# A decoder layer with grouped experts on one core: expert rows in blocks of 32 instead of 64

## The chip, the cores and the metric

The kernel runs on one core of a Trainium2 chip. One launch computes the whole layer for one sequence of 512 positions, all in fp32. The metric is the device time of that launch in microseconds (us); lower is better. Three runs of the kernel before are given.

Engines: PE is TensorE (its weight loads are shown apart, as PEld), DVE is VectorE, ACT is ScalarE, POOL is GpSimd, and SP is SyncE, which here issues the loads of the weights.

## The reference, cut to what matters

The layer is a mixer (attention heads of several kinds) followed by a mixture of experts. The change lies in the second part: each of the 512 rows is sent to two of 16 experts of one group.

```python
def grouped_moe(u, w_router, w1, w3, w2):
    aff = softmax(xt @ w_router)                       # 512 x 16
    group_score = top_k(aff by groups of 4, 2).sum(-1)
    g_sel = argmax(group_score)                        # one of 4 groups
    top_w, top_i = top_k(aff inside the group, 2)      # two experts, weights sum to 1
    ...
    for e in range(16):
        h = silu(xt @ w1[e]) * (xt @ w3[e])            # 1024 -> 512
        y = y + gate[:, e:e + 1] * (h @ w2[e])         # 512 -> 1024
x = x + g2 * grouped_moe(rms_norm(x, norm2) * (1 + sc2) + sh2, ...)
```

There are 1024 pairs of a row and an expert. Each expert has three matrices, w1 and w3 of 1024 x 512 and w2 of 512 x 1024, 6.29 MB together.

## The kernel before, in words

The first 557 us of the launch are the modulation, the input projection, the attention branches, the output projection and the router. They are the same in both kernels, but for the shape of one copied tile (gate2).

The expert stage starts when DVE has counted how many rows each expert gets. Experts get whole blocks of BT = 64 rows, at least one block each; `block_start` holds the running number of blocks, and `expert_rows` in DRAM holds the rows by expert, with room for padding. GpSimd scatters the normalised rows there. Then all engines walk over the blocks, in loops whose bounds are read from `block_start` at run time. For one block g:

- ACT's queue loads the rows into `xg` (64 partitions, one buffer) by `xg_load`, line 633.
- PE transposes `xg` in 8 pieces into banks 4 and 5 (`xg_T`, line 1516); DVE and ACT copy four pieces each into `xgT`, with the scale and shift of the modulation (lines 1148 and 639).
- First product (`inner`, line 1523): the 64 rows are the stationary operand, so a product fills only half of the array's columns. Two products, h = 0 and 1, go to column tiles at partitions 0 and 64 and take different columns of w1 and w3. It is done in two halves s, each 8 k x 2 tiles of 256 columns.
- For each half: silu on ACT (line 645), product with the other half on DVE (line 1155), transpose on PE (line 1529), copy on ACT (line 649).
- Second product (`outer`, line 1535): 2 x 2 products of 512 columns for each half, again in two column tiles. DVE multiplies the result by the gate row into `y_sb` (line 1160), and GpSimd's queue stores it in two DMAs (line 759) over the rows that it came from.

Order on PE inside a block: first product of half 0, half of that of half 1, transpose of half 0, the rest of half 1, four row transposes of the next block, second product of half 0, transpose of half 1, the other four row transposes, second product of half 1. Before the last k of the first product PE waits until the rows of the next block are in `xg` (semaphore s_xg). `xg_load(g + 2)` is the last thing in ACT's block: it waits for the transposes of block g + 1 (m_xt_v).

The weights of three experts fit into SBUF. SP loads those of expert e + 3 into the place of expert e: w1 and w3 when the first product of e's last block is done (m_h1), w2 when its second product is done (m_y). After the last block GpSimd gathers two rows per position and DVE adds them to the residual, weighted (lines 764, 1170, 1172), and SP stores the output.

## Time and profile before

| | us |
|---|---|
| median of 3 runs | 904.97 |
| lowest, highest | 899.85, 905.54 |
| the profiled execution | 905.1 |
| its span, first to last instruction | 903.5 |
| PE busy | 759.6 (84%) |
| DVE busy, ACT busy | 314.7, 236.9 |
| mean granted clock of PE | 0.895 |

The profiled execution is one more run, taken with the profiler; its span begins with the first instruction. Busy times of different engines overlap, so they do not add up to the span. A row with many records under one line adds up their union, so records that run side by side count once. In the timeline a row is a group of neighbouring instructions: start, length, engine, line, operation, names and shapes, count, and in brackets how long the engine was idle before and what ended that. The fp32 products appear as two records each.

### The profile page before, as it was taken

The numbers are of one execution on the slowest core, as the hardware profiler recorded it, in microseconds if no ns is written. First come the engines' busy times: TensorE is split into PE (matmuls) and PEld (weight loads), VectorE is DVE, ScalarE is ACT, GpSimd is POOL, SyncE is SP. The second block draws the span as 40 slices with busy tenths as digits, with TensorE's granted clock in tenths as the row PEclk, the third lists the DMA queues.
The fourth block names the chain that finished last, engine by engine and source line by source line (L and its number), as shares of the span: only waits on it lengthen the run. The fifth ranks groups of instructions, "written<-read, shape, count | busy, mean of one in ns | idle before, by whom it ended". The sixth has DMA issues, their size and how long they took to land.

```text
span 903.5 us, 11767 instructions
## 1 busy us (share of the span) xinstructions
PE 759.6 (84%) x4258; PEld 461.0 (51%) x4259; DVE 314.7 (35%) x743; ACT 236.9 (26%) x609; POOL 79.3 (9%) x148
## 2 busy tenths in 40 slices
PE   0599999787999999777799861999999999999970
PEld 0544555545666666556544460555555555555530
DVE  3635254221546566463423531112121211211114
ACT  2011001042334444344311300223332223323220
POOL 5010000151000000000000003000000000000013
PEclk9689999868589999978799955999999999999995
DMA  8785623512990000000090345499999999998117
GB/s 319 283 335 187 232 110 124 166 30 83 331 242 20 0 0 0 1 1 0 0 357 15 116 164 209 126 368 373 380 379 378 375 376 377 385 373 313 46 46 279
DMA packets 74488, 178.42 MB, mean 197 GB/s; under 512 B 5014, under 2 KB 19934, under 8 KB 71390
## 3 DMA queue, kind: packets, MB, share of 16 engines
q1 hardware_dynamic: 65328, 152.90, 47.6%
q0 software_dynamic: 4736, 14.95, 4.7%
q10 hardware_dynamic: 4400, 10.25, 3.8%
q8 instruction: 14, 0.23, 0.1%
q14 instruction: 10, 0.08, 0.0%
HBM read 156.33 MB, written 21.76 MB: 197 GB/s over the span
## 4 chain that ended last, share of the span: by engine, by line
PE 80%; DVE 7%; ACT 4%; DMA 3%; issue 3%; POOL 2%; SPq 0%; POOLq 0%; ACTq 0%; DVEq 0%
PE score L1523 20%; PE bank L1216 13%; PE score L1535 10%; PE score L1447 6%; PE bank L1314 5%; PE score L1335 4%; PE bank L1306 3%; PE bank L1516 2%; PE bank L1390 2%; DVE pool_sb L794 2%; PE bank L1259 2%; PE score L1487 1%; PE bank L1529 1%; ACT pool_sb L550 1%; PE bank L1379 1%
## 5 line engine op out<-in xcount | busy, mean ns | idle before, releaser
L1523 PE MATMUL score<-pool_sb,featT 128*64 128x256 f32 x1600 | 184.7, 384 | 5.5 <-issue 3.2
L1523 PEld LDWEIGHTS score<-pool_sb,featT 128*64 128x64 f32 x1600 | 122.4, 138 | 67.9 <-issue 23.2
L1216 PE MATMUL bank<-pool_sb,featT 128*128 128x512 f32 (+2 forms) x320 | 114.9, 522 | 2.9 <-DVE pool_sb L821 1.9
L1535 PE MATMUL score<-pool_sb,featT 128*64 128x512 f32 x400 | 96.9, 605 | 0.0
L1216 PEld LDWEIGHTS bank<-pool_sb,featT 128*128 128x128 f32 x320 | 61.8, 194 | 55.7 <-issue 49.8
L1155 DVE TENSOR_TENSOR featT<-featT,score 128x128 f32<-128x128 f32 x50 | 14.4, 288 | 176.2 <-ACT featT L645 176.2
L794 DVE SCALAR_TENSOR_TENSOR pool_sb<-pool_sb,cond 128x2048 f32<-128x2048 f32 x24 | 56.3, 2348 | 1.8 <-DMA pool_sb<-in_ada_w 0.6
L1447 PE MATMUL score<-pool_sb,featT 128*128 128x512 f32 x128 | 56.7, 603 | 0.0
L1148 DVE TENSOR_SCALAR featT<-bank,mod_col 128x64 f32<-128x64 f32 x104 | 28.6, 336 | 74.8 <-PE bank L1516 74.8
L759 POOL DMA_DIRECT2D expert_rows<-featT x50 | 26.2, 524 | 298.8 <-DVE featT L1160 297.1
L550 ACT ACTIVATE pool_sb<-score,nmax 128x128 f32<-128x128 f32 (+3 forms) x64 | 33.1, 522 | 72.4 <-PE bank L1306 63.5
L1335 PE MATMUL score<-pool_sb 66*128 66x128 f32 (+3 forms) x128 | 51.2, 515 | 0.0
L1314 PE MATMUL bank<-pool_sb 128*64 128x128 f32 x320 | 45.2, 293 | 6.5 <-ACT pool_sb L532 4.9
L645 ACT ACTIVATE featT<-score 128x128 f32<-128x128 f32 x50 | 13.8, 277 | 126.6 <-PE score L1523 126.6
L1314 PEld LDWEIGHTS bank<-pool_sb 128*64 128x64 f32 x320 | 37.3, 146 | 18.3 <-issue 11.2
L1516 PE MATMUL bank<-ident,featT 64*128 64x64 f32 x208 | 24.1, 238 | 20.8 <-DMA featT<-expert_rows 20.8
L639 ACT ACTIVATE featT<-bank,mod_col 128x64 f32<-128x64 f32 x104 | 33.5, 402 | 30.3 <-PE bank L1516 27.7
L1535 PEld LDWEIGHTS score<-pool_sb,featT 128*64 128x64 f32 x400 | 24.3, 136 | 33.1 <-issue 28.5
L949 DVE TENSOR_REDUCE nmax<-score 128x2 f32<-128x256 f32 (+3 forms) x32 | 26.3, 822 | 39.9 <-PE score L1337 39.9
L1447 PEld LDWEIGHTS score<-pool_sb,featT 128*128 128x128 f32 x128 | 24.5, 194 | 30.2 <-issue 29.7
L645 ACT ACT_TABLE_LOAD x25 | 32.1, 1283 | 26.3 <-PE bank L1516 24.4
L1516 PEld LDWEIGHTS bank<-ident,featT 64*128 64x128 f32 x208 | 17.0, 141 | 33.5 <-DMA featT<-expert_rows 20.9
(257 smaller groups left out, 832.9 us busy)
## 6 DMA issues: line engine op xcount, KB each, us to landing
pool_sb<-in_moe_w SPq DMA_DIRECT2D x48, 2048.0 KB, 19.7
...
```

Source lines behind the costliest of these rows:

```text
L550: ins = nc.scalar.activation(probs[:, 2 * b + r, 0:w], S2[b][:, r, 0:w], ACT.Exp, bias=nmax[:, b, r:r + 1], accum_out=sums[:, b, r:r + 1])
L639: m = nc.scalar.activation(xgT[:, 4 + k, :], banks[5][:, k * BT:(k + 1) * BT], ACT.Identity, scale=mod_col[:, 20 + k:21 + k], bias=mod_col ...
L645: nc.scalar.activation(silu[:, s, :], banks[s][:, 0:P], ACT.Silu).then_inc(m_si, 1)
L794: nc.vector.scalar_tensor_tensor(out=acc[:, g % 2, :], in0=stage[:, n % 3, :], scalar=cond[:, k:k + 1], in1=acc[:, g % 2, :], op0=ALU.mult ...
L1148: m = nc.vector.tensor_scalar(xgT[:, k, :], banks[4][:, k * BT:(k + 1) * BT], mod_col[:, 16 + k:17 + k], mod_col[:, 24 + k:25 + k], ALU.mu ...
L1216: m = nc.tensor.matmul(banks[4 + i][:, 0:n], featT[:, k, i * P:(i + 1) * P], w_stage[:, g % 3, k, 0:n], start=(k == 0), stop=(k == KD - 1))
L1314: m = nc.tensor.matmul(banks[6][b * DH:(b + 1) * DH, q * P:(q + 1) * P], proj[:, k, V_COL[r] + b * DH:V_COL[r] + (b + 1) * DH], probsT[:, ...
L1335: nc.tensor.matmul(S2[b][:, r, 0:w], qT[0:AUG, b, q * P:(q + 1) * P], kT[0:AUG, 2 * r + b, 0:w], start=True, stop=False)
L1447: m = nc.tensor.matmul(banks[2 * (j % 2) + g], featT[:, 4 * g + k, i * P:(i + 1) * P], w_out_sb[:, 4 * g + k, h], start=(k == 0), stop=(k ...
L1516: m = nc.tensor.transpose(banks[4 + k // 4][:, (k % 4) * BT:(k % 4 + 1) * BT], xg[:, k * P:(k + 1) * P], ident[0:BT, 0:BT])
L1523: mm = nc.tensor.matmul(banks[s][h * BT:(h + 1) * BT, 0:2 * P], xgT[:, k, :], w13[:, :, k, at0:at0 + P], start=(k == 0), stop=(k == KD - 1))
L1535: mm = nc.tensor.matmul(banks[2][h * BT:(h + 1) * BT, :], hT[:, s, c * BT:(c + 1) * BT], w2[:, 2 * c + s, h * 512:(h + 1) * 512], start=(s ...
```

## The change

A block has BT = 32 rows, and each expert gets at least two blocks. The stationary operand has 32 columns, so four products go to four column tiles (NT = 4) at partitions 0, 32, 64 and 96. The hidden width of 512 is split over the four tiles, so the first product is no longer done in halves: 8 k x 4 tiles of 256 columns into one bank, and one silu, one product, one transpose and one copy per block. The second product is 4 x 4 products of 256 columns; the result is 128 x 256, and one DMA stores it. DVE copies five of the eight transposed pieces, ACT three.

The second product of a block now stands behind the first product of the next one. `outer` waits also until DVE has read the bank of the block before (m_ye). The last block's result has its own buffer `y_last`. ACT issues `xg_load(g + 2)` ahead of its scaled copies, once all eight transposes are done (m_xt).

```diff
@@ -34,8 +34,11 @@
 W_GROUPS = [(0, 512), (512, 512), (1024, 280), (1304, 512), (1816, 256)]
 
 R_QN, R_QS, R_KSL, R_KW, R_KS, N_R = 0, 8, 16, 18, 20, 22
-BT = 64
-MAXB = (2 * T) // BT + NE - 1
+BT = 32
+NT = P // BT
+HB, DN = DE // NT, D // NT
+MIN_BLOCKS = 2
+MAXB = (2 * T) // BT + MIN_BLOCKS * NE
 N_ROWS = -(-(MAXB + 2) * BT // P) * P
@@ -175,10 +177,11 @@
         blkbuf = featT[:, :, :].rearrange("p k n -> p (k n)")
         xg = blkbuf[0:BT, 0:D]
         xgT = blkbuf[:, D:D + KD * BT].rearrange("p (k n) -> p k n", k=KD)
-        y_sb = blkbuf[:, 2 * D:2 * D + D // 2]
-        silu = blkbuf[:, 3 * D:3 * D + HB].rearrange("p (s n) -> p s n", s=2)
-        hmid = blkbuf[:, 3 * D + HB:3 * D + 2 * HB].rearrange("p (s n) -> p s n", s=2)
-        hT = blkbuf[:, 3 * D + 2 * HB:3 * D + 3 * HB].rearrange("p (s n) -> p s n", s=2)
+        silu = blkbuf[:, 2 * D:2 * D + HB]
+        hmid = blkbuf[:, 2 * D + HB:2 * D + 2 * HB]
+        hT = blkbuf[:, 2 * D + 2 * HB:2 * D + 2 * HB + P]
+        y_sb = blkbuf[:, 3 * D:3 * D + DN]
+        y_last = blkbuf[:, 3 * D + DN:3 * D + 2 * DN]
 
         yab = ring[:, :, 0:TT * D].rearrange("p b (i n) -> p b i n", i=TT)
         xs = nc.dram_tensor("expert_rows", (N_ROWS, D), F32, kind="Internal").ap()
@@ -432,8 +434,8 @@
             load_matrix(2, 0)
             sp.wait_ge(t_gs, 1)
             for e in range(NE - 3):
-                hi = sp.value_load(block_start[0:1, e + 1:e + 2], min_val=1, max_val=MAXB)
-                sp.wait_ge(m_h1, hi * 2)
+                hi = sp.value_load(block_start[0:1, e + 1:e + 2], min_val=MIN_BLOCKS, max_val=MAXB)
+                sp.wait_ge(m_h1, hi)
                 load_matrix(e + 3, 0)
                 load_matrix(e + 3, 1)
                 sp.wait_ge(m_y, hi)
@@ -634,35 +636,29 @@
 
             def xg_T(g):
 
-                act.wait_ge(m_xt_a, g + 1)
-                for k in range(4):
-                    m = nc.scalar.activation(xgT[:, 4 + k, :], banks[5][:, k * BT:(k + 1) * BT], ACT.Identity,
-                                             scale=mod_col[:, 20 + k:21 + k], bias=mod_col[:, 28 + k:29 + k])
+                for k in range(3):
+                    m = nc.scalar.activation(xgT[:, 5 + k, :], banks[5][:, k * BT:(k + 1) * BT], ACT.Identity,
+                                             scale=mod_col[:, 21 + k:22 + k], bias=mod_col[:, 29 + k:30 + k])
                 m.then_inc(m_xa, 1)
 
-            def silu_half(g, s):
-                act.wait_ge(m_h1, g * 2 + (s + 1))
-                nc.scalar.activation(silu[:, s, :], banks[s][:, 0:P], ACT.Silu).then_inc(m_si, 1)
-
-            def hT_half(g, s):
-                act.wait_ge(m_ht, g * 2 + (s + 1))
-                nc.scalar.activation(hT[:, s, :], banks[6 + s][:, 0:P], ACT.Copy).then_inc(m_hT, 1)
+            def block_of_rows(g):
+                act.wait_ge(m_h1, g + 1)
+                nc.scalar.activation(silu, banks[0][:, 0:HB], ACT.Silu).then_inc(m_si, 1)
+                act.wait_ge(m_xt, g + 2)
+                xg_load(g + 2)
+                xg_T(g + 1)
+                act.wait_ge(m_ht, g + 1)
+                nc.scalar.activation(hT, banks[6][:, 0:P], ACT.Copy).then_inc(m_hT, 1)
 
             act.wait_ge(s_scat, 16 * 2 * TT)
             xg_load(0)
+            act.wait_ge(m_xt, 1)
+            xg_load(1)
             xg_T(0)
-            act.wait_ge(m_xt_v, 1)
-            xg_load(1)
             act.wait_ge(t_gs, 1)
             total = all_blocks(act)
             with act.Fori(0, total) as g:
-                silu_half(g, 0)
-                hT_half(g, 0)
-                silu_half(g, 1)
-                xg_T(g + 1)
-                hT_half(g, 1)
-                act.wait_ge(m_xt_v, g + 2)
-                xg_load(g + 2)
+                block_of_rows(g)
             act.wait_ge(s_xg, total * 16 + 32)
             nc.scalar.activation(ssq2, ssq2, ACT.Copy)
 
@@ -753,11 +749,15 @@
 
             pool.wait_ge(t_gs, 1)
             total = all_blocks(pool)
-            with pool.Fori(0, total) as g:
-                pool.wait_ge(m_ye, g + 1)
-                for h in range(2):
-                    pool.dma_start(xs[bass.ds(g * BT, BT), h * 512:(h + 1) * 512], y_sb[h * BT:(h + 1) * BT, :]).then_inc(s_ys, 16)
-            pool.wait_ge(s_ys, total * 32)
+
+            def store_rows(y, g):
+                pool.wait_ge(m_ye, g + 2)
+                pool.dma_start(xs[bass.ds(g * BT, BT), :].rearrange("r (h n) -> h r n", h=NT), y).then_inc(s_ys, 16)
+
+            with pool.Fori(0, total - 1) as g:
+                store_rows(y_sb, g)
+            store_rows(y_last, total - 1)
+            pool.wait_ge(s_ys, total * 16)
             nc.gpsimd.tensor_tensor(descend, descend, descend, ALU.mult)
             for i in range(TT):
                 for b in range(2):
@@ -1120,7 +1122,7 @@
             dve.wait_ge(r_rank, 1)
             dve.wait_ge(t_const, 2)
...
             tot = banks[1][:, TT * NE:TT * NE + NE]
-            ch(nc.vector.tensor_scalar(nb, tot, 1.0, 1.0 / BT, ALU.max, ALU.mult))
+            ch(nc.vector.tensor_scalar(nb, tot, (MIN_BLOCKS - 1) * BT + 1.0, 1.0 / BT, ALU.max, ALU.mult))
             ch(nc.vector.tensor_scalar(nb, nb, 0.5 - 0.5 / BT, ROUND, ALU.add, ALU.add))
             ch(nc.vector.tensor_scalar(nb, nb, -ROUND, None, ALU.add))
             ch(nc.vector.tensor_tensor(gsm, tri16, nb.unsqueeze(1).broadcast_to([P, NE + 1, NE]), ALU.mult))
@@ -1143,27 +1145,34 @@
                 ch(nc.vector.tensor_tensor(wab[:, b * TT:(b + 1) * TT], wab[:, b * TT:(b + 1) * TT], wsum, ALU.mult))
 
             def xg_T(g):
-                dve.wait_ge(m_xt_v, g + 1)
-                for k in range(4):
+                dve.wait_ge(m_xt, g + 1)
+                for k in range(5):
                     m = nc.vector.tensor_scalar(xgT[:, k, :], banks[4][:, k * BT:(k + 1) * BT], mod_col[:, 16 + k:17 + k],
                                                 mod_col[:, 24 + k:25 + k], ALU.mult, ALU.add)
                 m.then_inc(m_xv, 1)
 
-            def block_of_rows(g, first):
-                for s in range(2):
-                    dve.wait_ge(m_si, g * 2 + (s + 1))
-                    nc.vector.tensor_tensor(hmid[:, s, :], silu[:, s, :], banks[s][:, P:2 * P], ALU.mult).then_inc(m_h, 1)
+            def rows_out(y, g, stored):
+                dve.wait_ge(m_y, g + 1)
+                if stored:
+                    dve.wait_ge(s_ys, g * 16)
+                nc.vector.tensor_tensor(y, banks[2][:, 0:DN], gate2_part[:], ALU.mult).then_inc(m_ye, 1)
+
+            def block_of_rows(g):
+                dve.wait_ge(m_si, g + 1)
+                nc.vector.tensor_tensor(hmid, silu, banks[0][:, HB:2 * HB], ALU.mult).then_inc(m_h, 1)
                 xg_T(g + 1)
-                if not first:
-                    dve.wait_ge(s_ys, g * 32)
-                dve.wait_ge(m_y, g + 1)
-                nc.vector.tensor_tensor(y_sb, banks[2], gate2_half[:], ALU.mult).then_inc(m_ye, 1)
-
+
+            nc.vector.memset(y_sb[0:1, 0:1], 0.0).then_inc(m_ye, 1)
             xg_T(0)
-            block_of_rows(0, True)
+            block_of_rows(0)
             dve.wait_ge(t_gs, 1)
-            with dve.Fori(1, all_blocks(dve)) as g:
-                block_of_rows(g, False)
+            total = all_blocks(dve)
+            block_of_rows(1)
+            rows_out(y_sb, 0, False)
+            with dve.Fori(1, total - 1) as g:
+                block_of_rows(g + 1)
+                rows_out(y_sb, g, True)
+            rows_out(y_last, total - 1, False)
 
             for i in range(TT):
                 dve.wait_ge(c_g[i], 32)
@@ -1511,59 +1520,63 @@
                     m = nc.tensor.matmul(banks[1][:, o], tri_b[:], mcount[:, o], start=(i == 0), stop=True)
             m.then_inc(r_rank, 1)
 
-            def xg_T(k0, done):
-                for k in range(k0, k0 + 4):
-                    m = nc.tensor.transpose(banks[4 + k // 4][:, (k % 4) * BT:(k % 4 + 1) * BT], xg[:, k * P:(k + 1) * P], ident[0:BT, 0:BT])
-                m.then_inc(done, 1)
-
-            def inner(w13, s, ks):
-                for k in ks:
-                    for h in range(2):
-                        at0 = h * HB + s * P
-                        mm = nc.tensor.matmul(banks[s][h * BT:(h + 1) * BT, 0:2 * P], xgT[:, k, :], w13[:, :, k, at0:at0 + P],
+            def xg_T():
+                for k in range(KD):
+                    at0 = (k % 5) * BT
+                    m = nc.tensor.transpose(banks[4 + k // 5][:, at0:at0 + BT], xg[:, k * P:(k + 1) * P], ident[0:BT, 0:BT])
+                m.then_inc(m_xt, 1)
+
+            def inner(slot, g):
+                pe.wait_ge(m_xa, g + 1)
+                pe.wait_ge(m_xv, g + 1)
+                for k in range(KD):
+                    if k == KD - 1:
+                        pe.wait_ge(s_xg, g * 16 + 32)
+                    for h in range(NT):
+                        mm = nc.tensor.matmul(banks[0][h * BT:(h + 1) * BT, 0:2 * HB], xgT[:, k, :], exp_w13[slot][:, :, k, h * HB:(h + 1) * HB],
                                               start=(k == 0), stop=(k == KD - 1))
-                return mm
-
-            def hT_half(g, s):
-                pe.wait_ge(m_h, g * 2 + (s + 1))
-                nc.tensor.transpose(banks[6 + s][:, 0:P], hmid[:, s, :], ident[:]).then_inc(m_ht, 1)
-
-            def outer(g, w2, s):
-                pe.wait_ge(m_hT, g * 2 + (s + 1))
-                for c in range(2):
-                    for h in range(2):
-                        mm = nc.tensor.matmul(banks[2][h * BT:(h + 1) * BT, :], hT[:, s, c * BT:(c + 1) * BT],
-                                              w2[:, 2 * c + s, h * 512:(h + 1) * 512], start=(s == 0 and c == 0),
-                                              stop=(s == 1 and c == 1))
-                return mm
-
-            def expert(e, b, n):
-                w13, w2 = exp_w13[b], exp_w2[b]
-                with pe.Fori(*blocks_of(pe, e)) as g:
-                    pe.wait_ge(e_w13[b], n * 32 + 32)
-                    pe.wait_ge(m_xa, g + 1)
-                    pe.wait_ge(m_xv, g + 1)
-                    inner(w13, 0, range(KD)).then_inc(m_h1, 1)
-                    inner(w13, 1, range(4))
-                    hT_half(g, 0)
-                    inner(w13, 1, range(4, 7))
-                    pe.wait_ge(s_xg, g * 16 + 32)
-                    inner(w13, 1, range(7, KD)).then_inc(m_h1, 1)
-                    xg_T(4, m_xt_a)
-                    pe.wait_ge(e_w2[b], n * 16 + 16)
-                    outer(g, w2, 0)
-                    hT_half(g, 1)
-                    xg_T(0, m_xt_v)
-                    outer(g, w2, 1).then_inc(m_y, 1)
+                mm.then_inc(m_h1, 1)
+
+            def outer(g, slot):
+                pe.wait_ge(m_hT, g + 1)
+                pe.wait_ge(m_ye, g + 1)
+                for c in range(NT):
+                    for h in range(NT):
+                        mm = nc.tensor.matmul(banks[2][h * BT:(h + 1) * BT, 0:DN], hT[:, c * BT:(c + 1) * BT],
+                                              exp_w2[slot][:, c, h * DN:(h + 1) * DN], start=(c == 0), stop=(c == NT - 1))
+                mm.then_inc(m_y, 1)
+
+            def inner_T(g):
+                pe.wait_ge(m_h, g + 1)
+                nc.tensor.transpose(banks[6][:, 0:P], hmid, ident[:]).then_inc(m_ht, 1)
+
+            def stage_of(g, slot, slot_before, uses):
+                pe.wait_ge(e_w13[slot], uses * 32)
+                inner(slot, g)
+                xg_T()
+                pe.wait_ge(e_w2[slot], uses * 16)
+                outer(g - 1, slot_before)
+                inner_T(g)
+
+            def expert(e, slot, uses):
+                lo, hi = blocks_of(pe, e)
+                stage_of(lo, slot, (slot + 2) % 3, uses)
+                with pe.Fori(lo + 1, hi) as g:
+                    stage_of(g, slot, slot, uses)
 
             pe.wait_ge(s_xg, 16)
-            xg_T(4, m_xt_a)
-            xg_T(0, m_xt_v)
+            xg_T()
+            pe.wait_ge(e_w13[0], 32)
+            inner(0, 0)
+            xg_T()
+            inner_T(0)
             pe.wait_ge(t_gs, 1)
+            with pe.Fori(1, blocks_of(pe, 0)[1]) as g:
+                stage_of(g, 0, 0, 1)
             with pe.Fori(0, NE // 3) as n:
-                for b in range(3):
-                    expert(n * 3 + b, b, n)
-            expert(NE - 1, 0, NE // 3)
+                for j in range(3):
+                    expert(n * 3 + (j + 1), (j + 1) % 3, n + (1 + j // 2))
+            outer(all_blocks(pe) - 1, 0)
 
 
 _INS = ['x', 'c', 'w_router', 'ada_w', 'ada_b', 'norm1_g', 'norm2_g', 'w_in', 'w_out', 'nsa_q_gain', 'nsa_k_gain',
```

On PE, first the end of the first product up to the second product of the second half, in the loop over the blocks of one expert. `featT` here is the buffer that holds xg, xgT, hmid and hT; `pool_sb` holds the weights. Before:

```order
L1550 ISA
L1523 MATMUL score<-pool_sb,featT 64x256 [waits s_xg]
L1523 MATMUL score<-pool_sb,featT 64x256
L1516 MATMUL bank<-ident,featT 128x64 x4
L1553 ISA
L1535 MATMUL score<-pool_sb,featT 64x512 [waits m_hT,e_w2_1]
L1535 MATMUL score<-pool_sb,featT 64x512 x3
L1528 REGISTER_ALU
L1529 MATMUL bank<-ident,featT 128x128 [waits m_h]
L1516 MATMUL bank<-ident,featT 128x64 x4
L1535 MATMUL score<-pool_sb,featT 64x512 [waits m_hT]
L1535 MATMUL score<-pool_sb,featT 64x512 x3
```

The whole block in the loop of the changed kernel:

```order
L1530 REGISTER_ALU [waits e_w13_1]
L1536 MATMUL score<-pool_sb,featT 32x256 [waits m_xv,m_xa]
L1536 MATMUL score<-pool_sb,featT 32x256 x27
L1534 ISA
L1536 MATMUL score<-pool_sb,featT 32x256 [waits s_xg]
L1536 MATMUL score<-pool_sb,featT 32x256 x3
L1526 MATMUL bank<-ident,featT 128x32 x8
L1545 MATMUL score<-pool_sb,featT 32x256 [waits m_ye,m_hT,e_w2_1]
L1545 MATMUL score<-pool_sb,featT 32x256 x15
L1551 MATMUL bank<-ident,featT 128x128 [waits m_h]
```

All eight row transposes stand together, and the wait for the next rows (s_xg) stands ahead of the last four products in both, once per block.

On ACT, the loop over the blocks before:

```order
L645 ACT_TABLE_LOAD
L645 ACTIVATE featT<-score 128x128 [waits m_h1]
L649 ACTIVATE featT<-bank 128x128 [waits m_ht]
L644 REGISTER_ALU
L645 ACTIVATE featT<-score 128x128 [waits m_h1]
L637 REGISTER_ALU
L639 ACTIVATE featT<-bank,mod_col 128x64 [waits m_xt_a]
L639 ACTIVATE featT<-bank,mod_col 128x64 x3
L649 ACTIVATE featT<-bank 128x128 [waits m_ht]
L633 ISA [waits m_xt_v]
L633 DMA featT<-expert_rows 64x1024
```

And in the changed kernel:

```order
L646 ACT_TABLE_LOAD
L646 ACTIVATE featT<-score 128x128 [waits m_h1]
L647 REGISTER_ALU
L635 ISA [waits m_xt]
L635 DMA featT<-expert_rows 32x1024
L640 ACTIVATE featT<-bank,mod_col 128x32 x3
L651 ACTIVATE featT<-bank 128x128 [waits m_ht]
```

The load of the rows stands ahead of the scaled copies now, behind one silu.

## Rows read from the trace of the kernel before

**Rows 1.** The page's costliest group: busy us, mean ns, idle before.

```profile
L1523 PE MATMUL score<-pool_sb,featT 128*64 128x256 f32 x1600 | 184.7, 384 | 5.5 <-issue 3.2
```

**Rows 2.** Windows of 20 us: busy time of each engine, clock, DMA.

```profile
core 0: us, PE busy (x) PEld busy (x) DVE busy (x) ACT busy (x) POOL busy (x), PEclk, DMA share, GB/s
605.00:625.00 20.00, 20.00 (x150) 10.79 (x148) 3.17 (x10) 6.08 (x17) 1.04 (x2) 1.00 1.04 373
825.00:845.00 20.00, 19.89 (x151) 11.22 (x149) 4.28 (x13) 5.52 (x12) 2.08 (x4) 1.00 0.46 159
```

**Rows 3.** Timeline of PE, one block and its neighbours: start us, us.

```profile
589.58 5.40 PE L1523 MATMUL score<-pool_sb,featT 128*64 128x256 f32 x48 [0.17 <-issue]
...
602.15 5.40 PE L1523 MATMUL score<-pool_sb,featT 128*64 128x256 f32 x48 [0.21 <-issue]
...
607.74 1.95 PE L1523 MATMUL score<-pool_sb,featT 128*64 128x256 f32 x16
...
609.62 0.46 PE L1516 MATMUL bank<-ident,featT 64*128 64x64 f32 x4
...
610.01 1.94 PE L1535 MATMUL score<-pool_sb,featT 128*64 128x512 f32 x8
...
611.88 0.33 PE L1529 MATMUL bank<-ident,featT 128*128 128x128 f32 x1
...
612.14 0.46 PE L1516 MATMUL bank<-ident,featT 64*128 64x64 f32 x4
...
612.58 1.94 PE L1535 MATMUL score<-pool_sb,featT 128*64 128x512 f32 x8
...
614.34 5.35 PE L1523 MATMUL score<-pool_sb,featT 128*64 128x256 f32 x48
```

**Rows 4.** The same timeline: the other engines at that block's end.

```profile
610.12 1.29 ACT L639 ACTIVATE featT<-bank,mod_col 128x64 f32<-128x64 f32 x4
...
612.63 1.10 DVE L1148 TENSOR_SCALAR featT<-bank,mod_col 128x64 f32<-128x64 f32 x4 [2.31 <-PE bank L1516]
612.77 0.48 ACTq L633 DMA_DIRECT2D featT<-expert_rows  x1
...
614.56 0.69 DVE L1160 TENSOR_TENSOR featT<-score,gate_half 128x512 f32<-128x512 f32 x1 [0.82 <-PE score L1535]
615.91 1.12 POOL L759 DMA_DIRECT2D expert_rows<-featT  x2 [11.46 <-DVE featT L1160]
618.01 0.28 ACT L645 ACTIVATE featT<-score 128x128 f32<-128x128 f32 x1 [3.15 <-PE score L1523]
618.32 0.29 DVE L1155 TENSOR_TENSOR featT<-featT,score 128x128 f32<-128x128 f32 x1 [3.07 <-ACT featT L645]
```

**Rows 5.** Timeline of PE in the router: small bf16 products.

```profile
539.92 0.25 PE L1508 MATMUL score<-mcount,ones_b 128*128 128x16 bf16 x4
```

**Rows 6.** Line 633, row loads: window 585:833, then 834:880.

```profile
L633 ACTq DMA_DIRECT2D featT<-expert_rows x20: 476/476/477, 587.7 to 825.0; - x20
DMA to landing us min/median/max: 6.2/6.4/7.1
...
DMA to landing us min/median/max: 3.4/3.4/3.4
```

**Rows 7.** Line 759, row stores, in the same two windows.

```profile
L759 POOL DMA_DIRECT2D expert_rows<-featT x40: 521/521/527, 590.8 to 828.7; - x40
DMA to landing us min/median/max: 4.2/5.7/7.7
...
DMA to landing us min/median/max: 2.2/2.3/2.4
```

**Rows 8.** Timeline: the first product of the stage and its end.

```profile
563.43 6.88 PE L1523 MATMUL score<-pool_sb,featT 128*64 128x256 f32 x48 [1.36 <-DVE featT L1148]
...
874.14 1.94 PE L1535 MATMUL score<-pool_sb,featT 128*64 128x512 f32 x8
...
876.12 0.69 DVE L1160 TENSOR_TENSOR featT<-score,gate_half 128x512 f32<-128x512 f32 x1 [0.82 <-PE score L1535]
```

20 lines of the change are left out of this document (10 added, 10 removed).

## The prediction

> **What bounds the kernel now.** I read the windows of 20 us first, then the order of time of one block, then the waits of the row transfers. The page's largest line is the first expert product, 1600 records of 384 ns that lie on one another in 184.7 us [rows 1]. The windows show the expert stage: from 585 to about 834 us TensorE is busy for 19 to 20 us in each 20, at full granted clock (1.00, 2.4 GHz), and the DMA engines are full too (share 1.04, 373 GB/s); in 825:845 their share is 0.46, which is 0.46/1.04 x 20 = 9 us of traffic, so the last weights land at about 834 us, and from then TensorE works alone until 876 us [rows 2, 8]. So TensorE bounds the stage, and the weights follow it closely.
>
> One block of 64 rows takes 12.19 us inside an expert (602.15 to 614.34) and 12.57 across a change of expert (589.58 to 602.15) [rows 3]. In the 5.35 us row 48 records stand, two for each fp32 product and the two column tiles together, so 24 steps; less the last record's own 0.38 us that is (5.35 - 0.38)/23 = 0.216 us a step [rows 1, 3], in which both tiles of 64 columns stream 256 columns each. Two tiles run fully side by side. The stage is 563.43 to 876.08 us (last product's start 874.14 plus 1.94), 312.7 us for 25 blocks [rows 8].
>
> **How many blocks there will be.** The reference's routing on its inputs gives the experts 82, 21, 65, 50, 56, 96, 43, 77, 69, 41, 15, 75, 87, 118, 78 and 51 rows. In blocks of 64 that is 25, as the trace has it. In blocks of 32, at least two each, it is 3 2 3 2 2 3 2 3 3 2 2 3 3 4 3 2 = 42 (1344 rows instead of 1600).
>
> **The block's price on TensorE.** First product: 8 x 4 products of 256 columns in four tiles, 8 x 2 steps x 0.216 = 3.45 us if all four run side by side; the trace has two tiles, not four. Ends: 3.45 (four together) and 6.9 (two and two). I take 3.45, since with two tiles nothing at all is lost. The change to transposes costs 0.15 (607.74 to 609.62 is 1.88 for 8 steps, 1.73) [rows 3]: 3.60. Eight transposes: four take 0.44 with the way back (612.14 to 612.58), eight between 0.44 and 0.88, I take 0.70. Second product: 4 x 2 steps of 256 columns, 1.73, plus 0.14, the same 1.87 that 610.01 to 611.88 shows for 4 steps of 512. Transpose of the middle: 0.26 (611.88 to 612.14). Sum 6.43, call it 6.4 us, against 12.1 for 64 rows: the same per row. 42 x 6.4 = 269 instead of 25 x 12.15 = 304.
>
> Issue: four tiles need a product record every 0.216/4 = 54 ns; four small bf16 products leave TensorE in 0.25 us [rows 5], so 62 ns or less each with the latency in it, and I cost issue at nothing. A change of expert costs 0.4 us now (12.57 less 12.19); its register loads stand behind the second product, of which 1.87 us now hide them and which will be queued at twice the records per us. Ends 0.4 and 1.5, I take 1.0: 15 us for 15 changes. Fill and drain of the new order (the second product runs one block late): 2 us at the start for copies that nothing covers, 0.8 at the end. TensorE alone: 563.4 + 269 + 15 + 2.8 = 850 us.
>
> **What hides.** Silu and the product with it need 0.28 + 0.29 [rows 4] and lie under 0.70 + 1.87. The scaled copies come after the transposes: DVE 5 x 0.275 = 1.4 us (four took 1.10 at twice the width), ACT a DMA issue of 0.48 and 3 x 0.32 = 1.4; under 1.87 + 0.26 [rows 3, 4]. Just covered; in any block in which they are not, tenths of a us are lost. The number of weights is the same.
>
> **The new wait: rows go round once per block.** There is still one buffer for gathered rows. The load for block g+2 is issued when the transposes of g+1 are done, and the last k of the next first product waits for it. Today 12 us lie between two loads and a load lands in 6.2 to 7.1 us under weight traffic, 3.4 without it [rows 6]: hidden. In the new block the round is: landing L, wake-up 0.1, two steps 0.43, mode change 0.15, transposes to their end about 0.7, then 0.17 to the issue (612.14 + 0.46 = 612.60 to 612.77) [rows 3, 4]: L + 1.5. For 32 rows L is not in the trace. Lower end 3.4 (a landing without traffic), upper 7.1. A load is 262 KB; at 373 GB/s that is 0.7 us, or 1.4 if it shares the engines evenly with weights; half of it saves 0.7, so L = 6.4 - 0.7 = 5.7 and the round is 7.2 us, longer than 6.4. **This, not TensorE, sets the pace while weights flow.** By a rule of the Trainium skill (DMA: Bandwidth & Descriptors, the fit of a fixed 2.0 us plus bytes over 436 GB/s) half the bytes save only 0.3 us. The trace's 3.4 us is above that fit and its 6.4 far above it, so the fit's fixed part does not hold here.
>
> The store has such a round too, since y_sb is one buffer: DVE's product of 256 columns (0.42, between 0.35 and 0.69), 0.66 to GpSimd (615.25 to 615.91), landing, 0.1. Stores of 131 KB land in 4.2/5.7/7.7 us under traffic and 2.3 without [rows 4, 7]. The new store has the bytes of one of today's two, in 1 KB pieces instead of 2 KB: 5.7 gives 6.9 us, the ends 5.4 and 8.9. Behind this wait stand DVE's next products and, through m_ye, the second product. I take 6.9, just below the load's round.
>
> **The sum.** Weights for 13 experts x 6.29 MB at 373 GB/s are 219 us, and some 35 blocks x 0.26 MB of rows 24 us: 243 us of full queues. Blocks in that time go at 7.2: 243/7.2 = 33.8; the other 8.2 at 6.4: 52.5. With 2.8 for fill and drain and 3.5 for those changes of expert that the round does not absorb: 563.4 + 301.8 = 865.2 us. An expert needs 16.8 + 2.6 x 0.7 = 18.7 us of DMA and 2.6 x 7.2 = 18.9 of its blocks, so they keep pace. At 6.4 a block they would still be in time: loads start when expert 0's third block is through its first product (563.4 + 2 + 2 x 6.4 + 3.6 = 582), so the last expert's first two matrices land at about 582 + 12 x 18.7 + 12.5 = 819, and TensorE reaches it at 563.4 + 2 + 40 x 6.4 + 14 = 835. Before, the stage ended at 876.1: -10.9. Behind it one store issue of two goes (about 0.6 of 1.12) and 0.27 of DVE [rows 4]: -0.9. The profiled execution took 905.1 us (span 903.5), the runs' median is 904.97, so both bases agree. 905 - 12 = **893 us**.
>
> **Rivals.** (a) Landing shrinks to 5.0 or less: the period is TensorE's 6.4, the stage ends at 850, time 878. For it: 3.4 us without traffic; against: traffic is there until about 825. Chance 0.18, 872 to 885.
> (b) Half the bytes hardly land sooner, L = 6.2 (the fastest of today under traffic) to 6.4: rounds of 7.7 to 7.9, by the same sum 907 to 913. For it: of 6.4 us at most 1.4 is transfer by the rate in [rows 2]. Chance 0.17, 903 to 915. With the 0.3 us of the fit named above (Trainium skill, DMA: Bandwidth & Descriptors) the round would be 7.6 and the time 905, an estimate by that page.
> (c) Slower: the store's round decides. Its 128 pieces of 1 KB land at today's worst 7.7, the round is 8.9; 243/8.9 = 27.3 blocks in traffic, 14.7 at 6.4, the stage ends at about 907, time 935. It decides from a store landing of 6.1 us, and the kernel is slower by 1% from about 6.7. For it: 7.7 occurs today; against: the median is 5.7. Chance 0.11, 915 to 937.
> (d) Four column tiles do not stream side by side. As two and two the block costs 6.4 + 3.45 + 1.73 = 11.6, 42 blocks 487 us, time about 1095. Or the loss is partial, 0.28 us a step, a third of the way to two and two: 24 x 0.065 more gives 8.0 a block, 42 x 8.0 + 18 = 354, stage end 917, time 945. Chance 0.09 in all. The Trainium skill (TensorE: Matmul & The Clock Gate, Measured speedup vs the span model) has 3.07 times for four row tiles and 2.38 for three column tiles, not 4 and 3; by that rate (4/3.07 x 0.216 = 0.28) the partial loss is the case. Here two tiles lose nothing, so the trace speaks against it.
> (e) Forecast, L of 5.4 to 6.0, 885 to 903: 0.42. The remaining 0.03 is anything else, such as TensorE waiting for weights.
>
> **Chances and range.** What a measurement here can tell from no change is about 1%, 9 us: faster is below 896, slower above 914. Faster: (a) 0.18 and some 0.29 of (e); same: 0.13 of (e) and nearly all of (b), 0.30; slower: (c), (d) and a rest, 0.23. The range leaves out the fastest of (a), (d) and the worst of (c): 874 to 925.
>
> **What will show it.** The profile after should have 42 stores and 42 silus; four first-product records per 0.216 us (64 in about 3.6 us); TensorE idle once per block, just before the last k of the first product, released by the DMA into featT, for 0.8 us while the DMA share is near 1 and for nothing after about 825 us; DVE waiting for the store in few blocks. No such idle time means (a); idle time ahead of DVE's last product released by expert_rows means (c); steps of 0.28 us or more mean (d). I am wrong if the block period under traffic is not between 6.9 and 7.5 us.

## The result and the profile after

The changed kernel takes 918.78 us (median of 4 runs, 915.0 to 922.38) where the kernel before takes 903.85 us (4 runs, the three above among them): a ratio of 1.0171 between their means, 95% interval 1.0112 to 1.0231. It is slower by 1.7%; the forecast was 893 us, faster by 1.3%.

The page of the kernel after: the shares of the chain of waits, the costliest groups of the expert stage, and two of the DMA groups (count, KB each, median us to landing).

```profile
span 914.9 us, 16431 instructions
...
PE 52%; DMA 27%; DVE 9%; issue 5%; ACT 4%; POOL 2%; POOLq 0%; SPq 0%; ACTq 0%; DVEq 0%
...
L1536 PE MATMUL score<-pool_sb,featT 128*32 128x256 f32 x2688 | 161.5, 390 | 18.0 <-DMA featT<-expert_rows 8.5
...
L1545 PE MATMUL score<-pool_sb,featT 128*32 128x256 f32 x1344 | 90.6, 414 | 25.9 <-DVE featT L1158 25.7
L1158 DVE TENSOR_TENSOR featT<-score,gate_part 128x256 f32<-128x256 f32 x42 | 17.9, 425 | 197.1 <-DMA expert_rows<-featT 187.7
...
featT<-expert_rows ACTq DMA_DIRECT2D x44, 128.0 KB, 5.3
expert_rows<-featT POOLq DMA_DIRECT2D x42, 128.0 KB, 6.9
```

Line 1536 is the first product, 1545 the second, 1158 DVE's product that writes the result buffer, and `expert_rows<-featT` the store of that buffer. DVE stood 187.7 of 197.1 us behind the store, and TensorE then 25.7 us behind DVE: the order of waits that rival (c) names. The chain of waits gives DMA 27% of the span; by line, 23% are this store. In the kernel before DMA had 3%.

The windows of 20 us of the kernel after:

```profile
core 0: us, PE busy (x) PEld busy (x) DVE busy (x) ACT busy (x) POOL busy (x), PEclk, DMA share, GB/s
605.00:625.00 20.00, 15.67 (x238) 8.98 (x242) 5.36 (x21) 6.70 (x16) 2.07 (x3) 0.95 1.03 363
685.00:705.00 20.00, 15.95 (x222) 8.57 (x218) 3.55 (x14) 6.34 (x13) 1.38 (x2) 0.83 1.04 355
705.00:725.00 20.00, 17.19 (x290) 10.02 (x286) 5.12 (x19) 6.28 (x15) 2.07 (x3) 1.00 0.81 270
825.00:845.00 20.00, 17.41 (x263) 9.88 (x266) 5.43 (x21) 6.71 (x16) 2.07 (x3) 0.91 0.82 286
```

In [rows 2] TensorE was busy for 19.9 to 20 of 20 us at a granted clock of 1.00; now it is busy for 15.7 to 17.4. In 685:705 its granted clock is 0.83, a mean of stretches at 2.4 and at 1.2 GHz (in 699.7:703.0 it is 0.50). In 705:725 the DMA share is only 0.81: SP starts no load of weights from 703.4 to 714.3, waits there 10.0 us for a first product, and in 713:715 the share is 0.00. TensorE is so late that weights wait for a free buffer.

The timeline of the kernel after over two blocks (start us, us, engine, line; in brackets the idle time before and what ended it):

```profile
699.67 3.64 PE L1545 MATMUL score<-pool_sb,featT 128*32 128x256 f32 x32 [2.62 <-DVE featT L1158]
...
706.75 0.42 DVE L1158 TENSOR_TENSOR featT<-score,gate_part 128x256 f32<-128x256 f32 x1 [5.88 <-DMA expert_rows<-featT]
707.84 0.69 POOL L755 DMA_DIRECT2D expert_rows<-featT  x1 [6.97 <-DVE featT L1158]
...
707.89 0.68 PE L1526 MATMUL bank<-ident,featT 32*128 32x32 f32 x8
...
708.50 1.93 PE L1545 MATMUL score<-pool_sb,featT 128*32 128x256 f32 x32
...
710.62 3.66 PE L1536 MATMUL score<-pool_sb,featT 128*32 128x256 f32 x64
...
712.95 0.42 DVE L1158 TENSOR_TENSOR featT<-score,gate_part 128x256 f32<-128x256 f32 x1 [3.16 <-DMA expert_rows<-featT]
...
714.21 0.68 PE L1526 MATMUL bank<-ident,featT 32*128 32x32 f32 x8
...
720.66 0.43 DVE L1158 TENSOR_TENSOR featT<-score,gate_part 128x256 f32<-128x256 f32 x1 [4.54 <-DMA expert_rows<-featT]
```

The round of the result buffer is 6.20 us (706.75 to 712.95) and then 7.71 (to 720.66). The block that nothing holds up takes 714.21 - 707.89 = 6.32 us, and its 64 first-product records end in 3.66 us, (3.66 - 0.38)/15 = 0.219 us a step of four records, one in each column tile (a record is half an fp32 product): four column tiles run side by side. After 2.62 us of idleness the second product takes 3.64 instead of 1.93 us: the granted clock had fallen to 0.50.

The row loads and the row stores of the kernel after, under weight traffic (565:820) and, for the stores, at its end and behind it (820:890; the weights end at about 841 us); they answer to [rows 6] and [rows 7]:

```profile
L635 ACTq DMA_DIRECT2D featT<-expert_rows x32: 322/322/332, 570.3 to 819.0; - x32
DMA to landing us min/median/max: 2.3/5.5/7.9
...
L755 POOL DMA_DIRECT2D expert_rows<-featT x31: 691/691/791, 573.2 to 819.3; - x31
DMA to landing us min/median/max: 4.0/7.1/9.1
...
DMA to landing us min/median/max: 3.8/4.2/5.9
```

Load and store carry the same 128 KB, and the store lands 1.6 us later. Today's store of as many bytes took 5.7 us under traffic and 2.3 without [rows 7]; this one takes 7.1 and 4.2. Its 31 issues stand (819.3 - 573.2)/30 = 8.20 us apart.

**Where the time went.** TensorE's part of the stage is 557.50 to 886.18 us, 328.7 us where [rows 8] give 312.7: +16.0. Behind it 28.7 us follow instead of 27.4, since the last store lands late: +1.3. The stage began 5.9 us sooner in the profiled run; its begin lies between 557.2 and 564.9 us over the nine profiles of the changed kernel and its variants, so that can be the spread of runs. Sum +11.4, the two spans' difference; the medians differ by 14.9.

### The profile page after: what moved, and what is told of

It reads as the page before. It is cut to its first block, busy times and chain, and to the rows that moved or that the text cites. A ratio compares the mean times of both kernels' runs of the same rounds, so it can differ in the third digit from the quotient of the medians.

```text
span 914.9 us, 16431 instructions
## 1 busy us (share of the span) xinstructions
PE 730.5 (80%) x6418; PEld 451.0 (49%) x6419; DVE 332.9 (36%) x866; ACT 260.1 (28%) x635; POOL 83.0 (9%) x140
## 3 DMA queue, kind: packets, MB, share of 16 engines
q10 hardware_dynamic: 4352, 8.94, 3.0%
## 4 chain that ended last, share of the span: by engine, by line
PE 52%; DMA 27%; DVE 9%; issue 5%; ACT 4%; POOL 2%; POOLq 0%; SPq 0%; ACTq 0%; DVEq 0%
DMA expert_rows<-featT 23%; PE bank L1225 12%; PE score L1456 6%; PE bank L1323 5%; PE score L1536 4%; PE score L1344 4%; PE bank L1315 3%; PE score L1545 2%; PE bank L1399 2%; PE bank L1268 2%; DVE featT L1158 2%; DVE pool_sb L794 2%; PE score L1496 1%; ACT pool_sb L552 1%; PE bank L1388 1%
## 5 line engine op out<-in xcount | busy, mean ns | idle before, releaser
L1536 PE MATMUL score<-pool_sb,featT 128*32 128x256 f32 x2688 | 161.5, 390 | 18.0 <-DMA featT<-expert_rows 8.5
L1536 PEld LDWEIGHTS score<-pool_sb,featT 128*32 128x32 f32 x2688 | 87.5, 112 | 78.2 <-DMA featT<-expert_rows 16.0
L1545 PE MATMUL score<-pool_sb,featT 128*32 128x256 f32 x1344 | 90.6, 414 | 25.9 <-DVE featT L1158 25.7
L1158 DVE TENSOR_TENSOR featT<-score,gate_part 128x256 f32<-128x256 f32 x42 | 17.9, 425 | 197.1 <-DMA expert_rows<-featT 187.7
L1545 PEld LDWEIGHTS score<-pool_sb,featT 128*32 128x32 f32 x1344 | 46.8, 116 | 50.6 <-issue 32.9
L755 POOL DMA_DIRECT2D expert_rows<-featT x42 | 29.2, 694 | 310.0 <-DVE featT L1158 291.5
L640 ACT ACTIVATE featT<-bank,mod_col 128x32 f32<-128x32 f32 x129 | 39.4, 375 | 61.1 <-PE bank L1526 61.1
L1150 DVE TENSOR_SCALAR featT<-bank,mod_col 128x32 f32<-128x32 f32 x215 | 50.9, 304 | 15.8 <-PE bank L1526 15.8
L1323 PE MATMUL bank<-pool_sb 128*64 128x128 f32 x320 | 43.1, 283 | 6.5 <-ACT pool_sb L534 5.0
L1526 PE MATMUL bank<-ident,featT 32*128 32x32 f32 x344 | 29.5, 226 | 19.6 <-DMA featT<-expert_rows 19.6
L646 ACT ACTIVATE featT<-score 128x128 f32<-128x128 f32 x42 | 11.7, 278 | 110.5 <-PE score L1536 110.5
L1526 PEld LDWEIGHTS bank<-ident,featT 32*128 32x128 f32 x344 | 24.7, 138 | 37.0 <-DMA featT<-expert_rows 19.7
```

The lines of the kernel that those rows point to most:

```text
L640: m = nc.scalar.activation(xgT[:, 5 + k, :], banks[5][:, k * BT:(k + 1) * BT], ACT.Identity, scale=mod_col[:, 21 + k:22 + k], bias=mod_col ...
L646: nc.scalar.activation(silu, banks[0][:, 0:HB], ACT.Silu).then_inc(m_si, 1)
L1150: m = nc.vector.tensor_scalar(xgT[:, k, :], banks[4][:, k * BT:(k + 1) * BT], mod_col[:, 16 + k:17 + k], mod_col[:, 24 + k:25 + k], ALU.mu ...
L1323: m = nc.tensor.matmul(banks[6][b * DH:(b + 1) * DH, q * P:(q + 1) * P], proj[:, k, V_COL[r] + b * DH:V_COL[r] + (b + 1) * DH], probsT[:, ...
L1526: m = nc.tensor.transpose(banks[4 + k // 5][:, at0:at0 + BT], xg[:, k * P:(k + 1) * P], ident[0:BT, 0:BT])
L1536: mm = nc.tensor.matmul(banks[0][h * BT:(h + 1) * BT, 0:2 * HB], xgT[:, k, :], exp_w13[slot][:, :, k, h * HB:(h + 1) * HB], start=(k == 0) ...
```

## The experiments

Theory A: the store's new access pattern has four pieces in its outermost dimension, its data goes over few DMA engines, and so it lands late; with one result buffer its round paces the blocks. Rivals: the 1 KB pieces are slow whatever their order (B, the reason that rival (c) gave); or the load's round or TensorE paces them and the store is no more than what ends last. The table puts the results together. "Result products" is the time from DVE's first result product to its last, divided by their number less one; it leaves out all that stands ahead of the stage. Landing is the store's under traffic, by the median. The ratio is to the runs of the kernel before that belong to that comparison (medians 902.06 to 905.58 us), so it is not the quotient of two medians of the table. e1, e5 and e7 do not compute the layer and stand for their time alone.

| kernel | us, median | ratio to before, 95% | result products, us | landing |
|---|---|---|---|---|
| before | 903.85 | | 298.8/24 = 12.45 | 5.7 |
| after | 918.78 | 1.0171 (1.0112 to 1.0231) | 314.1/41 = 7.66 | 7.1 |
| e1 contiguous store | 881.23 | 0.9755 (0.9705 to 0.9804) | 279.1/41 = 6.81 | 5.5 |
| e2 four stores | 911.66 | 1.0065 (1.0037 to 1.0093) | 305.7/41 = 7.46 | 5.0 |
| e3 two result buffers | 889.61 | 0.9858 (0.98 to 0.9915) | 281.3/41 = 6.86 | 7.1 |
| e4 before, one store | 945.12 | 1.0445 (1.0383 to 1.0507) | 337.3/24 = 14.05 | 13.4 |
| e5 = e1 and e3 | 883.11 | 0.9747 (0.9694 to 0.9799) | 275.5/41 = 6.72 | 5.5 |
| e6 = e3, request behind copies | 887.36 | 0.9819 (0.976 to 0.9878) | 282.0/41 = 6.88 | 7.2 |
| e7 = e3, no row loads | 868.75 | 0.9606 (0.9562 to 0.965) | 262.0/41 = 6.39 | 6.8 |
| e8 = e2 and e3 | 881.28 | 0.9738 (0.9694 to 0.9782) | 276.0/41 = 6.73 | 4.9 |
| e9 = e3, request later | 1006.74 | 1.117 (1.1117 to 1.1223) | 399.0/41 = 9.73 | 8.0 |

**e1: the same bytes in 128 pieces of one dimension.**

```diff
-pool.dma_start(xs[bass.ds(g * BT, BT), :].rearrange("r (h n) -> h r n", h=NT), y).then_inc(s_ys, 16)
+pool.dma_start(xs[bass.ds(g * BT, BT), :].rearrange("r (h n) -> (r h) n", h=NT), y).then_inc(s_ys, 16)
```

> The changed kernel, but the store of a block writes its 128 pieces of 1 KB one behind the other in DRAM (outermost dimension 128), not by row and quarter (outermost dimension 4). Same bytes, same pieces, same single DMA; the rows land in the wrong order, so the output's expert part is not the reference's. Theory A (the store's outermost dimension of 4 puts its data on 4 of the 16 DMA engines): the landing falls from 7.1 to about 5.5 us under weight traffic and from 4.2 to under 3 without; DVE hardly waits for it; the load round of 7.0 us sets the pace; time 893 to 903. Theory B (pieces of 1 KB are slow to write): landing and time as in the changed kernel, 7.1 us and 919. If the load round alone had cost the time, the time would also stay near 915.

Measured 881.23 us, below the range of theory A and far below that of B: the row load, too, landed sooner, in 5.2 us where the changed kernel has 5.5, and the stage took 6.81 us a block. DVE's waits for the store came to 9.1 us under traffic, not 172.4. The store of e1, under traffic and then behind it:

```profile
L755 POOL DMA_DIRECT2D expert_rows<-featT x36: 539/539/598, 572.9 to 817.1; - x36
DMA to landing us min/median/max: 2.0/5.5/6.5
...
DMA to landing us min/median/max: 2.0/2.0/2.0
```

Pieces of the same size, one dimension instead of two: 7.1 becomes 5.5 us under traffic and 4.2 becomes 2.0 without. So B is dead. The rate in 40 slices of 0.1 us shows the transfer itself, for one store without traffic, with the packets of GpSimd's queue in that window; first the kernel after (879:883; the bytes of the last three slices are the next load's), then e1 (849:853):

```profile
GB/s 0 0 0 0 0 0 0 3 48 46 1 41 0 41 0 0 0 0 0 0 82 123 41 164 82 82 164 41 123 123 82 41 0 0 0 0 0 164 205 164
...
q0 software_dynamic: 144, 0.13, 15.3%
```

```profile
GB/s 0 0 0 0 0 0 0 0 0 0 0 0 0 0 0 451 410 287 164 0 0 0 0 0 0 0 0 0 0 0 0 0 0 0 0 0 0 0 0 0
...
q0 software_dynamic: 48, 0.13, 9.2%
```

In e1 the store is over in 0.4 us; in the kernel after it drips for some 2.5, with three times as many packets for the same bytes. The queue of GpSimd (packets, MB, share of 16 engines) over the whole launch, on the pages of the kernel after and of e1:

```profile
q0 software_dynamic: 8384, 13.97, 4.6%
```

```profile
q0 software_dynamic: 4352, 13.91, 4.3%
```

The difference is 4032 packets for 42 stores, 96 each; the trace's packet records give them 16 bytes each. 128 KB in packets of 4 KB are 32. If four engines carry them, 8 each, and each of the other twelve goes through the same number of nearly empty ones, that makes 12 x 8 = 96. e4 tests this count.

The packet records (start and length of each) also show the spread directly. Between 585 and 835 us the changed kernel has at most four data packets of its stores under way at once in all but 0.3 of the 68.5 us in which there are any; e4 has at most two in all but 0.8 of 118.5 us; in e1 there are eight or more, up to 19, in 12.4 of 28.6 us.

**e2: four stores, one for each column tile.**

```diff
+for h in range(NT):
+    pool.dma_start(xs[bass.ds(g * BT, BT), h * DN:(h + 1) * DN], y[h * BT:(h + 1) * BT, :]).then_inc(s_ys, 16)
```

> The changed kernel, with four stores per block, one for each quarter of the columns, each of 32 rows x 1 KB (outermost dimension 32), instead of one. Theory A: each uses all 16 engines and lands in about 5.5 us, but the last is issued some 1.8 us after the first, so the store's round is 0.4 + 0.7 + 1.8 + 5.5 + 0.1 = 8.5 us against 8.3 now: time 912 to 922 under traffic-bound pace, though blocks without traffic have 2.3 us landings. Theory B: landings stay 7 us, round over 10, time 940 or more.

Measured 911.66 us, at the lower edge of what A expected. Each store lands in 5.0 us, but four issues stand in the round. The pieces of each are 1 KB, 4 KB apart in DRAM as in the changed kernel, so what e1 gained is not owed to its 128 KB lying in one run. The timeline of e2:

```profile
700.66 0.42 DVE L1159 TENSOR_TENSOR featT<-score,gate_part 128x256 f32<-128x256 f32 x1 [6.05 <-DMA expert_rows<-featT]
...
701.75 2.24 POOL L756 DMA_DIRECT2D expert_rows<-featT  x4 [5.58 <-DVE featT L1159]
...
708.48 0.42 DVE L1159 TENSOR_TENSOR featT<-score,gate_part 128x256 f32<-128x256 f32 x1 [5.88 <-DMA expert_rows<-featT]
```

The round is 7.82 us: 0.42, 0.67 to GpSimd, 2.24 for the issues, the rest the last store's landing. What the landing gains, the issues nearly use up.

**e3: the store as it is, two result buffers in turn.** The loops of DVE and GpSimd go by two blocks, with a semaphore for each buffer; this takes an even number of blocks for granted, here 42.

```diff
-            with pool.Fori(0, total - 1) as g:
-                store_rows(y_sb, g)
+            with pool.Fori(0, total, 2) as g:
+                store_rows(0, g)
+                store_rows(1, g + 1)
...
-                rows_out(y_sb, g, True)
+                rows_out(0, g, g * 8)
+                block_of_rows(g + 2)
+                rows_out(1, g + 1, g * 8)
```

> The changed kernel with its store as it is (four engines), but two result buffers that alternate, so that a store has two block times to land. Both A and B: landings stay about 7 us, DVE's wait for the store disappears, the row load's round (landing 5.5 plus 1.5) is left as the limit: block under traffic 7.0 to 7.2 us instead of 8.1, time 890 to 900. Rival (the weights bound the stage now, or the load round does): time stays above 910.

Measured 889.61 us, at the lower edge of the expected range. The store still lands in 7.1 us and DVE no longer waits for it. The timeline of e3, and its window:

```profile
705.47 0.64 PE L1548 MATMUL score<-pool_sb,featT 128*32 128x256 f32 x8 [0.40 <-DMA featT<-expert_rows]
...
706.04 0.68 PE L1538 MATMUL bank<-ident,featT 32*128 32x32 f32 x8
...
706.89 0.32 ACTq L636 DMA_DIRECT2D featT<-expert_rows  x1
...
712.96 0.68 PE L1538 MATMUL bank<-ident,featT 32*128 32x32 f32 x8
```

```profile
685.00:705.00 20.00, 19.22 (x315) 10.76 (x307) 5.66 (x21) 8.25 (x18) 2.06 (x3) 1.00 1.05 365
```

Now the block takes 6.92 us (706.04 to 712.96) with one short stall ahead of the last k, released by the row load, a clock of 1.00 and a DMA share of 1.05: the picture that the forecast drew for the changed kernel, with 6.9 for its 7.2.

**e4: the kernel before with one store of its 256 KB, two pieces in the outermost dimension.**

```diff
-                for h in range(2):
-                    pool.dma_start(xs[bass.ds(g * BT, BT), h * 512:(h + 1) * 512], y_sb[h * BT:(h + 1) * BT, :]).then_inc(s_ys, 16)
+                pool.dma_start(xs[bass.ds(g * BT, BT), :].rearrange("r (h n) -> h r n", h=2), y_sb).then_inc(s_ys, 16)
```

> The kernel before (64 rows), with its two stores per block made one, outermost dimension 2. Theory A: the 262 KB go over 2 DMA engines, 32 packets of 0.155 us each, so 5 us of transfer even without traffic: landing 7 us without and 12 to 14 with traffic, round 14 us, longer than the block's 12.2: slower, 925 to 950. Theory B: pieces of 2 KB as before, landing about 5.8 and 2.5 us, no wait, 904.

Measured 945.12 us: this one edit makes the kernel before 4.5% slower. Its store under traffic, its queue, and its wait:

```profile
DMA to landing us min/median/max: 8.5/13.4/15.7
```

```profile
q0 software_dynamic: 15536, 15.04, 5.2%
```

```profile
DVE featT L1159 <- DMA expert_rows<-featT: 123.5, 21, 9.6
```

In e1 a store has 32 + 16 = 48 packets (16 are its completion's), so 4352 - 42 x 48 = 2336 belong to other work. The 25 stores of e4 then have (15536 - 2336)/25 = 528 each: 64 data packets, 16, and 448 = 14 x 32. That is two engines with 32 packets each and fourteen idle ones. The 168 stores of 32 KB in e2 have (7712 - 2336)/168 = 32, that is 16 and 16 with no idle engine (7712 packets on its page's q0 row). The count fits for 4, 2 and 16, and the landing goes with it: 5.5 us with 128 in the outermost dimension, 7.1 with four, 13.4 with two at twice the bytes. The Trainium skill (DMA: Bandwidth & Descriptors, Why a DMA increments its semaphore by 16 and not by 1, "How many engines (k)") states the rule: the number of engines is the largest up to 16 that divides the outermost dimension of both sides, with an exception for some copies issued by GpSimd. The counts here and the packets under way agree with the rule and not with the exception; which engines carried the data no row here shows.

**e5: e1 and e3 together.**

> Two result buffers and the store in contiguous pieces over all engines, both at once (rows land in the wrong order, so the expert part of the output is not the reference's). If the store costs time only through DVE's wait, then with either cure there is nothing left to win: 880 to 890, between the two. If four busy engines also slow the weights and the row loads, it is as fast as the contiguous store alone, 878 to 884, and faster than two buffers alone by 5 or more.

Measured 883.11 us, beside e1's 881.23: once the store lands in 5.5 us a second result buffer brings nothing. But it is 6.5 us below e3, and every run of it is below every run of e3: the second case of the expectation. The store over few engines costs something besides DVE's wait, and the row load lands in 5.2 us here and in 5.5 in e3. The packet records (585 to 835 us) have only 12 to 14 packets of weights under way for 56 us in e3 and for 10 in e5, which fits weights held back on the store's engines; that this is the cause is not shown.

**e6: e3 with the request for the next rows behind ScalarE's scaled copies.** Before the change it stood later still, behind the copy of the hidden rows, too.

```diff
-                xg_load(g + 2)
                 xg_T(g + 1)
+                xg_load(g + 2)
```

> The kernel with two result buffers, but ACT issues the load of the next rows behind its scaled copies instead of ahead of them: 0.95 us later. If the row load's round sets the pace there (now 5.5 + 1.5 = 7.0 us), it becomes 8.0 us: by the sum 243/8.0 = 30.4 blocks in traffic instead of 34.5, 4.1 blocks x 6.3 us = 26 us more, time about 915. If the weights' rate sets the pace, no change, 890.

Measured 887.36 us against 889.61: no difference, and my expectation of 915 missed. The timeline of e6 shows why:

```profile
707.77 0.68 PE L1538 MATMUL bank<-ident,featT 32*128 32x32 f32 x8
...
708.49 0.38 ACT L641 ACTIVATE featT<-bank,mod_col 128x32 f32<-128x32 f32 x1 [0.30 <-PE bank L1538]
...
708.63 0.32 ACTq L636 DMA_DIRECT2D featT<-expert_rows  x1
708.76 0.64 ACT L641 ACTIVATE featT<-bank,mod_col 128x32 f32<-128x32 f32 x2
```

The request stands behind three copies in the code, and goes out at 708.63, while the first of them runs: 0.86 us behind the begin of the transposes, and in e3 it was 0.85. The copies do not hold back the request. So the run did not delay the load and told nothing of the load's round. It does tell that issuing the load ahead of the scaled copies, a part of the change, is worth nothing by itself in e3.

**e7: e3 without its row loads,** but for the first two.

> The kernel with two result buffers, but only the rows of the first two blocks are loaded; all later blocks transpose what is in the buffer (the expert part of the output is not the reference's). If the load's round sets the pace: TensorE's own 6.32 us a block and its changes of expert remain, the stage takes about 273 us instead of 296, time about 868. If the weights' rate is the limit at 7.0 us a block: 5.5 MB less traffic gives at most 5 to 10 us, time 880 to 886, and TensorE waits for pool_sb.

Measured 868.75 us, as the load's round expected. The timeline of e7, and its window:

```profile
699.77 0.68 PE L1537 MATMUL bank<-ident,featT 32*128 32x32 f32 x8
...
706.09 0.68 PE L1537 MATMUL bank<-ident,featT 32*128 32x32 f32 x8
```

```profile
685.00:705.00 20.00, 19.85 (x339) 11.76 (x331) 5.66 (x21) 8.26 (x19) 2.06 (x3) 1.00 1.05 391
```

Without loads the block is TensorE's 6.32 us with the weights at 391 GB/s and the stores still there. So the 6.9 us of e3 are not the weights' rate. But e7 also takes some 5 MB out of the traffic, so it does not prove alone that the round is the mechanism; e9 adds that.

**e8: e2 and e3 together,** four stores into two buffers: the version to which the experiments point.

> Two result buffers and four stores of one quarter each, all on 16 engines. GpSimd then issues for 2.1 us a block, which nothing waits for; landing 5 us. If spread matters beyond DVE's wait: 882 to 887, a bit faster than two buffers with one store; otherwise 890 as that, or 1 to 2 us slower for the three more issues after the last block.

Measured 881.28 us (ratio 0.9738): 2.6% faster than the kernel before, where the change is 1.7% slower. The four issues now stand outside every round. It is 8.3 us faster than e3, slightly more than expected for the case that the spread matters beyond DVE's wait; the row load lands in 5.2 us here, too.

**e9: e3 with the request truly later,** behind ScalarE's wait for the transpose of the hidden rows.

```diff
                 act.wait_ge(m_xt, g + 2)
-                xg_load(g + 2)
                 xg_T(g + 1)
                 act.wait_ge(m_ht, g + 1)
+                xg_load(g + 2)
```

> The kernel of e3 with the request for the next rows not behind ScalarE's scaled copies, where the run before showed that it still went out 0.18 us behind the transposes, but behind ScalarE's wait for the transpose of the hidden rows. In e3 that wait ends at about 708.85 us where the request stood at 706.89, so the request comes some 2.0 us later. Theory 1, the round of the row load sets the pace under traffic (landing 5.2 + 1.8 from landing to the next request = 7.0 us a block): a round of 9.0, over some 33 blocks 66 us, of which a shorter landing gives back some as the queues empty: 930 to 955 us (e3: 889.6), TensorE's wait on the load 3.5 to 4 us in some 33 blocks. Theory 2, the blocks under traffic are paced by the weights or by the queues' rate, and the wait on the load only shows which of the transfers happened to come last: the load has slack to lose, and the time stays within 885 to 900 us.

Measured 1006.74 us. The load has no slack to lose, so theory 2 is dead; but the loss against e3 is 117 us, where theory 1 gave 40 to 65. The loads of e9 (565:900), its waits, and a block of its timeline:

```profile
L636 ACTq DMA_DIRECT2D featT<-expert_rows x32: 322/322/342, 567.7 to 898.0; - x32
```

```profile
PEld score L1548 <- DMA featT<-expert_rows: 90.3, 26, 4.3
```

```profile
702.17 1.08 PE L1548 MATMUL score<-pool_sb,featT 128*32 128x256 f32 x8 [2.94 <-DMA featT<-expert_rows]
703.18 1.06 PE L1538 MATMUL bank<-ident,featT 32*128 32x32 f32 x8
...
704.17 3.64 PE L1557 MATMUL score<-pool_sb,featT 128*32 128x256 f32 x32
...
708.39 0.32 ACTq L636 DMA_DIRECT2D featT<-expert_rows  x1
```

Under traffic the requests stand (898.0 - 567.7)/31 = 10.65 us apart, not 9.0. After about 3 us of idleness TensorE works at the lower clock (its 8 records in 1.08 instead of 0.64 us, the second product in 3.64 instead of 1.93), and since the request now stands behind that second product, the slow clock lengthens the round that caused it: 708.39 - 702.17 = 6.2 us from landing to request. The intended delay of 2.0 us and the 1.71 that the second product gains come to 3.7, and 10.65 less e3's 6.92 is 3.73.

## Why the prediction was wrong

**The step that failed** is the term "The new store has the bytes of one of today's two, in 1 KB pieces instead of 2 KB: 5.7 gives 6.9 us". The landing is 7.1 us under traffic and the round 0.42 + 0.67 + 7.1 + 0.1 = 8.3; the stores stand 8.20 us apart. The bytes were right and pieces of 1 KB land no later than today's of 2 KB (e1 has 5.5 us, today's 5.7). What the step left out is that one DMA over four column tiles has an outermost dimension of 4, so that its data goes over four engines at a time. With the load's round at 7.2, the forecast stood on two rounds 0.3 us apart, one of which was priced by bytes alone. With DVE's wait gone and the store as it is (e3) 29.2 us come back, with the store over all engines as well (e8) 37.5.

**Rival (c)** named the place, the waits and the point from which it decides (6.1, slower by 1% from 6.7) rightly; only its reason, pieces at their worst, was wrong. With 8.3 in its own sum, 243/8.3 = 29.3 blocks under traffic and 12.7 x 6.4 behind it make a stage of 243 + 81.3 + 6.3 = 330.6 us, measured 328.7, and a time of 922 us, measured 918.8. That it comes so near is in part luck: the weights did not keep the queues full for 243 us but ended at about 841, and 34 of the 42 stores, not 29.3, were issued by then. A chance of 0.11 was little for a store whose access pattern the trace did not hold.

**The block on TensorE**, 6.43, is 6.32, with the first product in 3.6 as taken; rival (d) falls at once. The issue of four records per 0.22 us did cost nothing. A change of expert, put at 1.0 us where only TensorE counts, is nearer 0.2: the 41 steps of e7 take 262.0 us, 2.9 more than 41 x 6.32, over 15 changes.

**The load's landing**, 5.7, is 5.5 (5.2 in e1 and e8). Its round paces the stage as soon as the store's does not: e3 has 6.92 us, and TensorE's part of the stage there, 559.6 to 855.4, is 295.8 us against the 301.8 of the forecast. Rivals (a) and (b), which move this landing to 5.0 or 6.2, have 872 to 885 and 903 to 915 us, and e3 lies between them. So the forecast was right for a kernel that the change did not make. The fit of the Trainium skill (DMA: Bandwidth & Descriptors, Anatomy of one DMA — SWDGE (gpsimd) path) that the prediction set beside this landing is one for DMAs issued by GpSimd, and the load stands on ACT's queue; the forecast does not hang on it.

**The 0.9 us at the end** became a loss of 1.3: of this 2.2 us the late landing of the last store explains 1.9 (4.2 instead of 2.3 us).

**The clock** was taken as 1.00 throughout. It falls once TensorE idles: the second products take 90.6 us in all, and 81.2 in e3 (its page's line 1557), 9.4 more. How much of that lies under the store's round and how much on the path, these runs don't tell.
